# Half as many first keys kept as dense tiles, now with their U rows, and the gathers skip them

## The reference

```python
q = (h @ w_query).reshape(B, S, 8, 2, 128)                   # 8 heads, two halves of a query
scores = einsum('bshcd,hckd->bshck', q, sub_keys)            # 128 first and 128 second keys
s_top, i_top = lax.top_k(scores, 16)
cand = s_top[..., 0, :, None] + s_top[..., 1, None, :]       # 16 x 16 pairs
cand_idx = i_top[..., 0, :, None] * 128 + i_top[..., 1, None, :]
best, pos = lax.top_k(cand.reshape(..., 256), 16)            # 16 experts per token and head
expert_idx = take_along_axis(cand_idx, pos); gate = softmax(best)
u = take(expert_u, expert_idx); v = take(expert_v, expert_idx)   # rows of 16384 x 2048 tables
out = sum_k (gate * gelu(u_k . h)) * v_k                     # 128 experts per token
```

## Time and profile before

| what | value |
|---|---|
| median of the runs | 2015.78 us |
| the profiled execution, first to last instruction | 2008.7 us |
| busy: PE, DVE, POOL, ACT | 88%, 68%, 52%, 29% |
| moved by the DMA queues | 647.28 MB |
| read from HBM | 729.91 MB |
| mean granted TensorE clock | 0.953 |

### The profile page before, as it was taken

The page is one execution under the profiler, slowest core; times in us unless marked ns, Lnnn a source line. Parts: engine busy times, 40 slices in busy tenths (PEclk is TensorE's granted clock), DMA queues, the critical chain, the costliest instruction groups (busy, mean ns, idle before and its releaser), DMA issues.

```text
span 2008.7 us, 18796 instructions
## 1 busy us (share of the span) xinstructions
PE 1770.1 (88%) x6283; PEld 1122.4 (56%) x6283; DVE 1368.9 (68%) x2191; ACT 574.5 (29%) x1037; POOL 1040.7 (52%) x643
## 2 busy tenths in 40 slices
PE   7999999999999999875565578898887899999996
PEld 6888888888888898622222233344333554444442
DVE  5463453233334338999889887787888888888956
ACT  5445464345543520210111132233313740000001
POOL 5443343444332413575555565465555668877732
PEclk9999999999999999887778899999998899999999
DMA  8986454665555679999999999999999999999997
GB/s 211 241 177 148 142 189 152 192 196 180 169 164 173 204 263 403 384 411 420 418 419 417 402 420 419 414 413 414 403 415 391 401 369 408 409 414 386 409 421 308
DMA packets 157641, 647.28 MB, mean 322 GB/s; under 512 B 25894, under 2 KB 31086, under 8 KB 95598
## 3 DMA queue, kind: packets, MB, share of 16 engines
q0 software_dynamic: 73728, 450.98, 55.2%
q1 hardware_dynamic: 83824, 195.16, 30.9%
HBM read 729.91 MB, written 2.10 MB: 364 GB/s over the span
## 4 chain that ended last, share of the span: by engine, by line
PE 52%; DMA 18%; DVE 13%; issue 9%; POOL 7%; POOLq 0%; ACT 0%; DVEq 0%; SPq 0%; ACTq 0%
DMA u_ring<-in_peer_u_dram,idx 10%; PE acc L1583 10%; PE acc L1585 10%; PE acc L1584 10%; PE misc L1967 8%; PE acc L1967 8%; DMA u_high<-in_peer_u_dram,idx 3%; DVE u_ring L1425 3%; DMA u_mid<-in_peer_u_dram,idx 3%; DVE u_ring L1423 3%; POOL u_ring L595 3%; POOL v_high L602 1%; POOL u_mid L595 1%; DVE u_mid L1425 1%; DVE u_mid L1423 1%
## 5 line engine op out<-in xcount | busy, mean ns | idle before, releaser
L553 POOL TENSOR_TENSOR w_lo<-raw,w_hi 128x1024 fp32r<-128x1024 f32 x112 | 276.3, 2467 | 421.0 <-ACT w_hi L677 420.7
L1583 PE MATMUL acc<-w_hi,t_hi 128*128 128x512 f32 x896 | 355.0, 396 | 0.0
L1585 PE MATMUL acc<-w_hi,t_lo 128*128 128x512 f32 x896 | 349.3, 390 | 0.0
L1584 PE MATMUL acc<-w_lo,t_hi 128*128 128x512 f32 x896 | 348.9, 389 | 0.0
L1025 DVE TENSOR_TENSOR w_lo<-raw,w_hi 128x1024 fp32r<-128x1024 f32 x112 | 158.4, 1415 | 265.7 <-ACT w_hi L677 265.6
L595 POOL DMA_INDIRECT u_ring<-in_peer_u_dram,idx x160 | 210.2, 1314 | 249.0 <-DVE dots L1425 195.1
L677 ACT ACTIVATE w_hi<-raw 128x1024 fp32r<-128x1024 f32 x224 | 237.0, 1059 | 330.8 <-PE acc L1585 281.1
L1932 PE MATMUL misc<-v_high,diag 128*128 128x512 f32 x368 | 203.7, 705 | 87.0 <-DMA v_high<-in_peer_v_dram,idx 84.2
L1932 PE MATMUL misc<-v_low,diag 128*128 128x512 f32 x368 | 191.7, 670 | 79.1 <-DMA v_low<-in_peer_v_dram,idx 79.1
L1423 DVE CUSTOM_DVE_ANT_0 u_ring<-u_ring,hn 128x1024 f32<-128x1024 f32 x160 | 195.8, 1224 | 72.5 <-DMA u_ring<-in_peer_u_dram,idx 65.8
L1425 DVE CUSTOM_DVE_ANT_0 u_ring<-u_ring,hn 128x1024 f32<-128x1024 f32 x160 | 195.3, 1221 | 0.0
(11 more groups left out here) (286 smaller groups left out, 2433.4 us busy)
## 6 DMA issues: line engine op xcount, KB each, us to landing
u_ring<-in_peer_v_dram SPq DMA_DIRECT2D x48, 1024.0 KB, 8.9
raw<-in_w_in_dram SPq DMA_DIRECT2D x64, 512.0 KB, 7.0
raw<-in_xattn_wk_dram SPq DMA_DIRECT2D x32, 512.0 KB, 4.6
raw<-in_xattn_wv_dram SPq DMA_DIRECT2D x32, 512.0 KB, 3.9
raw<-in_w_out_dram SPq DMA_DIRECT2D x32, 512.0 KB, 4.7
raw<-in_xattn_wq_dram SPq DMA_DIRECT2D x32, 512.0 KB, 4.9
raw<-in_xattn_wo_dram SPq DMA_DIRECT2D x32, 512.0 KB, 4.8
praw<-in_peer_wq_dram SPq DMA_DIRECT2D x24, 512.0 KB, 8.6
```

The lines of the kernel that those rows point to most:

```text
L553: nc.gpsimd.tensor_tensor(w_lo[:, j % RING, :, :], raw[:, j % RING, :, :], w_hi[:, j % RING, :, :].bitcast(F32), ALU.subtract).then_inc(lo ...
L1583: nc.tensor.matmul(o, xh, w_hi[:, s, kk, :], start=first, stop=False)
L1584: nc.tensor.matmul(o, xh, w_lo[:, s, kk, :], start=False, stop=False)
L1585: ins = nc.tensor.matmul(o, xl, w_hi[:, s, kk, :], start=False, stop=last)
```

## The change

`DENSE` falls from 48 to 24, and the 24 dense first keys now hold for both tables and for all groups: U and V gathers skip rows of those keys. The scores of the dense rows come from TensorE. SP loads the 24 U tiles of 1 MB into two slots (`du`). PE turns a tile in four **units** of four 128x128 blocks, ACT copies a unit's result to `duT`, and PE multiplies it with the query block `t2f`, 256 tokens at once (four products, `dense_dots`). When a tile's four units are done, ACT writes the gelu of the 128 x 256 scores into `wT`. There are 96 units, 12 in each of groups 2 to 9. Since `t2f` isn't normed, DVE first scales it by 1/rms of each token, spread over the partitions by a PE product (`spread_scales`, `scale_queries`). The scatter now moves the gates instead of the weights, and DVE multiplies them into `wT` (`apply_gates`, in place of ACT's copy). Batches of chunk 0 run in groups 10 to 13, four in a period, and of chunk 1 in group 14 (4) and 15 (12).

Other edits that come with it: a dot is one operation over 2048 columns, and `sum_dots` is gone; skipped rows leave old data in a slot, so `weights` writes `low_wts` by a mask and a predicated copy over zeros; buffers are laid out anew. U has 5 slots in groups 2 to 9 and 7 from group 10 on, where the two new ones lie over `t2f`; V has 3 slots up to group 9 and 7 after that. The V gathers per group (`SHARES`) are 0, 4, then 5 in groups 2 to 9, then 10 or 11; the last 21 of chunk 0 move into the tail, one behind every third late row. DVE adds the late rows with every fourth from row 68 on left to PE.

```diff
-    DENSE = 48
-    WHOLE = 2
+    DENSE = 24
...
+    wT = (put("wT0", [P, DENSE, P], F32, at_v + 16 * KB), put("wT1", [P, DENSE, P], F32, at_raw + 24 * KB))
+    du = put("du", [P, 2, D], F32, at_raw)
+    duT = put("duT", [P, 4, CW], F32, at_raw + 16 * KB)
...
+        SHARES = (0, 4) + 8 * (5,) + 3 * (10, 11)
...
-            return n % 4 if n < 2 * TOP else (n - 2 * TOP + 4) % 7
+            if n < 2 * TOP:
+                return n % 4
+            return (4, 0, 1, 2, 3)[(n - 2 * TOP) % 5] if n < WIDE_U else (5, 6, 2, 3, 4, 0, 1)[(n - WIDE_U) % 7]
...
+        LATE_BATCHES = tuple((GROUPS - 2, k) for k in (9, 11, 13, 15)) + tuple((GROUPS - 1, k) for k in range(2, 14))
         def scatters(p, k):
+            if GATE_FROM <= p < LAST_GATES:
+                b = 4 * (p - GATE_FROM) + (k - 5) // 3
+                return range(b, b + 1) if k in (5, 8, 11, 14) else range(0)
+            if (p, k) in LATE_BATCHES:
+                b = BATCHES + LATE_BATCHES.index((p, k))
+                return range(b, b + 1)
+            return range(0)
+        UNITS = 4
+        def dense_units(p, k):
+            per = DENSE * UNITS // 8
+            if not 2 <= p < 10:
                 return range(0)
+            return range((p - 2) * per + k * per // TOP, (p - 2) * per + (k + 1) * per // TOP)
...
+            sp.wait_ge(peer_used, PC)
+            for e in range(DENSE):
+                if e >= 2:
+                    sp.wait_ge(duT_done, UNITS * (e - 1))
+                sp.dma_start(du[:, e % 2, :], u_rows[(FROM + e) * KEYS:(FROM + e + 1) * KEYS, :]).then_inc(tile_landed[e % 2], 16)
...
-                elif u_index(n) in (4, 5):
-                    pool.wait_ge(peer_used, PC)
-                elif n >= 2 * TOP:
+                elif u_index(n) > 4:
+                    pool.wait_ge(duT_used, UNITS * DENSE)
+                elif u_index(n) == 4:
...
+                    bounds_check=FROM * KEYS - 1, oob_is_err=False).then_inc(u_landed[u_index(n)], 16)
...
+                elif i < 3:
+                    pool.wait_ge(peer_used, PC - SLOTS + RING if n == 0 else PC)
+                elif i < 5:
+                    pool.wait_ge(duT_used, UNITS * DENSE)
...
+                if m % 3 == 2 and TAIL_V + m // 3 < TILE0:
+                    first_values(TAIL_V + m // 3)
...
+            def dense_unit(u):
+                act.wait_ge(duT_done, u + 1)
+                if u >= UNITS:
+                    act.wait_ge(duT_used, u - UNITS + 1)
+                nc.scalar.activation(duT[:, u % UNITS, :], acc[:, 0, u % 2, :], ACT.Copy).then_inc(duT_copied, 1)
+            def dense_gelu(x):
+                act.wait_ge(duT_used, UNITS * (x + 1))
+                for c in range(TT):
+                    ins = nc.scalar.activation(wT[c][:, x, :], acc[:, 1, x % 2, c * P:(c + 1) * P], ACT.Gelu)
+                ins.then_inc(pre_read, 1)
...
-                act.wait_ge(dots_summed, g + 1)
-                nc.scalar.activation(acts[:, q, :], dot_sums[:, q, :], ACT.Gelu, scale=rstd[:, c:c + 1]).then_inc(gelu_done, 1)
+                act.wait_ge(dot_done, g * TOP + TOP)
+                nc.scalar.activation(acts[:, q, :], dots[:, q, :], ACT.Gelu, scale=rstd[:, c:c + 1]).then_inc(gelu_done, 1)
...
+                    for u in dense_units(p, k):
+                        dense_unit(u)
+                        if u % UNITS == 1 and u > UNITS:
...
             def weights(g):
                 c, at = g // PH, slice(g % PH * TOP, (g % PH + 1) * TOP)
+                step(nc.vector.tensor_scalar(low_mask[:, :], lists[:, 0, c, at], float(FROM), None, ALU.is_lt))
+                dve.wait_ge(gated, g + 1)
                 dve.wait_ge(gelu_done, g + 1)
-                step(nc.vector.tensor_tensor(lists[:, 2, c, at], acts[:, g % 2, :], gate[:, g % 4, :], ALU.mult))
-                nc.vector.scalar_tensor_tensor(low_wts[:, g, :], lists[:, 0, c, at], float(FROM if g < GROUPS - WHOLE else KEYS), lists[:, 2, c, at],
-                                               ALU.is_lt, ALU.mult).then_inc(wts_ready, 1)
+                step(nc.vector.tensor_tensor(wts[:, :], acts[:, g % 2, :], lists[:, 2, c, at], ALU.mult))
+                nc.vector.copy_predicated(low_wts[:, g, :], low_mask[:, :], wts[:, :]).then_inc(wts_ready, 1)
+            def scale_queries():
+                dve.wait_ge(rstd_spread, 1)
+                nc.vector.tensor_tensor(t2f[:, :, :], t2f[:, :, :], acc[:, 1, 1, 0:S].unsqueeze(1).to_broadcast([P, KT, S]),
+                                        ALU.mult).then_inc(t2_scaled, 1)
+            def apply_gates(b):
+                c, t = b // BATCHES, b % BATCHES * WB
+                if b == 0:
+                    dve.wait_ge(pre_read, DENSE)
+                dve.wait_ge(wT_done, b + 1)
+                nc.vector.tensor_tensor(wT[c][:, :, t:t + WB], acc[:, 0, b % 2, 0:WB * DENSE].rearrange("p (t x) -> p x t", x=DENSE),
+                                        wT[c][:, :, t:t + WB], ALU.mult).then_inc(wT_copied, 1)
...
+                    nc.vector.tensor_tensor_reduce(out=row, in0=row, in1=hn[:, c, :], scale=1.0, scalar=0.0,
+                                                   op0=ALU.mult, op1=ALU.add, accum_out=dots[:, q, k:k + 1]).then_inc(dot_done, 1)
...
-            sum_dots(1, 1)
+            scale_queries()
...
+            def dense_dots(u):
+                x, b = u // UNITS, u % UNITS
+                if b == 0 and x >= 2:
+                    pe.wait_ge(pre_read, x - 1)
+                pe.wait_ge(duT_copied, u + 1)
+                for i in range(UNITS):
+                    kt = b * UNITS + i
+                    ins = nc.tensor.matmul(acc[:, 1, x % 2, 0:S], duT[:, u % UNITS, i * P:(i + 1) * P], t2f[:, kt, :], start=kt == 0, stop=kt == KT - 1)
+                ins.then_inc(duT_used, 1)
+            def dense_unit(u):
+                x, b = u // UNITS, u % UNITS
+                if b == 0:
+                    pe.wait_ge(tile_landed[x % 2], 16 * (x // 2 + 1))
+                if u >= 2:
+                    pe.wait_ge(duT_copied, u - 1)
+                for i in range(UNITS):
+                    ins = nc.tensor.transpose(acc[:, 0, u % 2, i * P:(i + 1) * P], du[:, x % 2, (b * UNITS + i) * P:(b * UNITS + i + 1) * P], ident[:, :])
+                ins.then_inc(duT_done, 1)
+                if u:
+                    dense_dots(u - 1)
...
+            pe.wait_ge(t2_scaled, 1)
             for p in range(2, GROUPS):
                 share = v_share(p)
                 for k in range(TOP):
+                    if p == GATE_FROM and k == 0:
+                        dense_dots(DENSE * UNITS - 1)
+                    if (p, k) in ((GATE_FROM, 1), (LAST_GATES, 7)):
+                        turn_lists(0 if p == GATE_FROM else 1)
                     for n in share[taken(p, k):taken(p, k + 1)]:
+                        take_values(n)
+                    for u in dense_units(p, k):
+                        dense_unit(u)
+                    for b in scatters(p, k):
+                        scatter_weights(b)
```

233 lines of the change are left out of this document (103 added, 130 removed).

## The result

The changed kernel takes 2099.67 us (median, 2094.37 to 2101.47 in 4 runs) against 2015.02 us for the kernel before on the same chip: a ratio of 1.0413, 95% interval 1.0391 to 1.0436. It is slower, as forecast, but by 85 us where the forecast was 24, and outside the range of 1994 to 2070. The profiled execution spans 2092.3 us, 83.6 more than the 2008.7 before.

| stage | before | after | difference | forecast |
|---|---|---|---|---|
| to the first dot of group 2 | 853.9 | 878.0 | +24.1 | +14 |
| groups 2 to 9, to the first dot of group 10 | 431.7 | 453.0 | +21.3 | +2 |
| groups 10 to 15, to the end of the dots | 352.6 | 369.9 | +17.3 | -6 |
| tail | 370.5 | 391.4 | +20.9 | +15 |

A forecast was written before the change was run, and what follows sets the result against it. Transfers were taken as the limit from 750 us on, with DVE next in groups 2 to 9 and PE in the tail. +16 to group 10, -6 and +15 gave +25: span 2034, time 2040; range 1994 to 2070.

The forecast's parts named there:

- Bytes: Whole kernel: 512 gathers of 0.857 MB move 438.6 MB, 12.4 MB fewer, worth 31 us at 405 GB/s.
- the sum of a period: Groups 2 to 9, each period: DVE work 46.1, a gelu wait of 3, and 3.7, giving 52.8 us; bounds 50.9 and 58.
- The wait for gelu: Groups 2 to 9: DVE's gate product waits 3 us each period for ACT's gelu, behind the last V row's units.
- The 3.7: Groups 2 to 9: last term added to each period's sum, 3.7 us, with no derivation given.
- POOL's lag of 2 to 4 us: Groups 2 to 9: gathers held by merged dots leave POOL 2 to 4 us late at each period's end.
- Start: To group 2's first dot: fourth V gather awaits PE's first take, then query scaling; +14 us, bounds +8 and +20.
- The 5.3: Before group 2: a gather takes 1.3 us at POOL and some 4 us to land with nothing queued.
- Group 9 to 10: Group 10's first U gather waits for all 96 units, so DVE stands 15 us (10 to 20).
- Groups 10 to 15: 138 MB at 402 GB/s take 343 us; group 15's PE work of 60 us and scatter waits add 3: -6 (-16 to +8).
- Tail: After group 15: 151 MB at 400 GB/s take 378 us, +15 (+5 to +22); PE bounds nothing.
- PE as the bound at 2082: Rival, groups 2 to 9: clock stays 0.82, PE sets periods of 58 us, +42, time 2082; chance 0.10.
- The 15 us that the rival put on the hold: Rival, groups 2 to 9: merged dots don't hold POOL, periods 50.9 us, time 2025, 15 less; chance 0.05.

## Why the prediction was wrong

- **Bytes:** right, 437.88 MB against 438.6. That they would be moved at 400 to 415 GB/s wherever no stop was forecast was wrong. Groups 3 to 8 ran at 384; groups 10 to 15 moved the forecast 138 MB at 372, not 402; only the tail came near (153.5 MB at 392, forecast 151 at 400).
- **Groups 2 to 9, +21 against +2:** the step that failed is the sum of a period, 46.1 + 3 + 3.7 = 52.8. DVE's own work of 46.1 was right: 55.2 less its waits is 46. The wait for gelu was forecast at 3 us and measured 0 to 1.1 (0.5 in the mean, DVE's idle time ahead of its gate product). The 3.7 is not derived in the prediction; it can stand for POOL's lag of 2 to 4 us or for DVE's waits for U rows, which were 3.0 to 3.9 before. The lag cost about nothing (next point), and the waits for U rows grew to 8.6. With 5 U and 3 V slots and skipped rows the queue does not stay full through DVE's searches, which the prediction had no term for. That the sum lay only 2.4 us below the 55.2 is in part luck, since one term was too large and the other too small.
- **POOL:** its lag beside merged dots is there (1.75 us a gather), but its price is about nothing (2.8 us in all, and 1.001 in the kernel before).
- **Start, +24 against +14:** the mechanism was right, and +24 lies beyond even the upper bound of +20. The second V gather's wait, named as the reason for +20, did come, since the chain from a late U row to PE's first take goes through DVE's routing and ACT: the fourth V gather was issued at 862.5, not 854.5. And the U gather behind it landed 7.6 us after its issue, not 5.3. The 5.3 holds for a gather with nothing in front of it (5.4 for that V gather, 5.3 for the first of group 10).
- **Group 9 to 10:** right, 18.7 against 15 and within its bounds.
- **Groups 10 to 15, +17 against -6:** groups 10 to 14 gave 2 us (294 against 296) of the 9 expected, and no run says why. Group 15 is the failure: PE's 60 us were counted at full clock and without waits, and "+3" was allowed for DVE's. PE was busy 68.6 us, at a mean clock of 0.84, and waited 7.3 more by ACT's order, 76 together; DVE's dots stood behind it. Removing the batches gave back 20.5.
- **Tail, +21 against +15:** within its bounds (and the forecast's own figures, 378 less 362, give +16). It starts in the third hole, 379 GB/s in the 25 us from 1700 on, and ends beside DVE's additions at 382 and less.
- **Rivals:** PE as the bound at 2082 is nearest in time, but its mechanism is refuted by the run without the units, and its condition wasn't met: PE was busy some 47 us a period at a clock of 0.94, where 53 were needed. The rule of the Trainium skill's page "SBUF — State Buffer", section "Who interferes with whom", as the prediction reads it, would not have a dot with both inputs in SBUF hold a gather; the page calls that inferred, for the writing of descriptors. These runs disagree (1.75 us beside merged dots, 1.25 beside halves). What the two contend for isn't shown: a gather also reads its indices from SBUF. The 15 us that the rival put on the hold were not there either.
- **Range:** it ended at 2070, though the upper bounds of the stages add up to far more. Four losses came together, two of them beyond their bounds (the start and groups 10 to 15).

## What to carry to other kernels

A rate read in a saturated stage holds only while as much is in flight: when a change makes requests smaller, look for the longest stretch in which no buffer is freed and compare it with what the queue holds. A gather put into an in-order queue with a new wait is priced by everything behind it; two such waits and one overlaid buffer cost 29 us here. Work that needs the last group's results falls into the last group's time: put it on the engines' timeline there, with the clock that the stage really had, before counting its products.
